# An encoder layer with 16 experts: where the prompt's matmuls stand between the sample's

## The reference, cut to what matters

```python
SEQ, DEC_SEQ, D_MODEL = 256, 1024, 1024          # prompt tokens, sample tokens
N_EXPERTS, CAPACITY_FACTOR, EXPERT_FF = 16, 2, 2048

def _expert_choice_ffn(h, w_router, w_e_gate, w_e_up, w_e_down):
    B, S, D = h.shape
    T = B * S
    cap = CAPACITY_FACTOR * T // N_EXPERTS       # 32 prompt rows, 128 sample rows per expert
    ht = h.reshape(T, D)
    aff = jax.nn.softmax((ht @ w_router).astype(jnp.float32), axis=-1)
    gate_vals, idx = lax.top_k(aff.T, cap)
    xe = ht[idx]
    hid = jax.nn.silu(jnp.einsum('ecd,edf->ecf', xe, w_e_gate)) * jnp.einsum('ecd,edf->ecf', xe, w_e_up)
    ye = jnp.einsum('ecf,efd->ecd', hid, w_e_down) * gate_vals[..., None].astype(h.dtype)
    out = jnp.zeros((T, D), ye.dtype).at[idx.reshape(-1)].add(ye.reshape(-1, D))
    return out.reshape(B, S, D).astype(h.dtype)

def _layer(x, ...):
    h = _rmsnorm(x, norm_mix)
    proj = h @ w_in
    ...
    o_a = _gla_branch(...)                       # gated linear attention, both directions
    o_b = _gqa_branch(...)                       # grouped-query attention
    merged = jax.nn.sigmoid(z_a) * (o_a @ w_o_gla) + jax.nn.sigmoid(z_b) * (o_b @ w_o_att)
    x = x + merged @ w_out
    x = x + _expert_choice_ffn(_rmsnorm(x, norm_ffn), w_router, w_e_gate, w_e_up, w_e_down)
    return x
```

## Time and profile before

| | us |
|---|---|
| median of 3 runs | 3241.99 |
| lowest and highest | 3238.33, 3242.4 |
| the profiled execution: its own time | 3243.4 |
| its span, first to last instruction | 3241.8 |
| TensorE busy in the span | 3032.2 (94%) |
| VectorE, ScalarE busy | 1706.0 (53%), 1518.9 (47%) |
| SP's loads and stores, share of the 16 DMA engines' span | 43.9% |
| sample matmuls, high weights times rows | 578.2, 395 ns each |
| prompt matmuls on the rows | 236.1, 383 ns each |

### The profile page before, as it was taken

One profiled execution on the slowest core, in us unless ns is written; L12 is line 12 of the kernel. 1 busy time (PEld: TensorE's weight loads), 2 busy tenths in 40 slices (PEclk: granted clock), 3 DMA queues, 4 the chain that ended last, 5 costly groups with the idle time before them and its releaser, 6 DMA issues. The chain is left out here.

```text
span 3241.8 us, 51622 instructions
## 1 busy us (share of the span) xinstructions
PE 3032.2 (94%) x19370; PEld 2396.0 (74%) x19370; DVE 1706.0 (53%) x1733; ACT 1518.9 (47%) x1647; POOL 564.5 (17%) x732
## 2 busy tenths in 40 slices
PE   7999998899987799988885999999999999999998
PEld 5888886777776689967773777777777777777776
DVE  3101000544443299942337666666766766666665
ACT  4211111455543166631443565656656655566554
POOL 0038883012210000000101000111110001111100
PEclk9999998999998899999996999999999999999999
DMA  4324322232325300034436778888877787888874
GB/s 147 131 97 142 117 89 95 92 108 86 95 73 194 110 14 20 13 120 173 143 122 226 273 278 304 282 286 297 293 272 279 281 304 277 289 299 286 277 278 151
DMA packets 196508, 600.83 MB, mean 185 GB/s; under 512 B 15360, under 2 KB 45712, under 8 KB 196432
## 3 DMA queue, kind: packets, MB, share of 16 engines
q1 hardware_dynamic: 165952, 507.51, 43.9%
q0 software_dynamic: 21760, 74.99, 7.8%
q10 hardware_dynamic: 8720, 17.30, 1.5%
HBM read 522.33 MB, written 77.33 MB: 185 GB/s over the span
## 5 line engine op out<-in xcount | busy, mean ns | idle before, releaser
L1932 DVE TENSOR_TENSOR ex_w_lo<-ex_w_raw,ex_w_hi 128x2048 fp32r<-128x2048 f32 x384 | 879.7, 2291 | 451.5 <-ACT ex_w_hi L1887 451.5
L1887 ACT ACTIVATE ex_w_hi<-ex_w_raw 128x2048 fp32r<-128x2048 f32 x381 | 730.0, 1916 | 469.5 <-PE ex_ps_s L2019 469.3
L2019 PE MATMUL ex_ps_s<-ex_w_hi,ex_xS 128*128 128x512 f32 x2048 | 578.2, 395 | 0.0
L2019 PEld LDWEIGHTS ex_ps_s<-ex_w_hi,ex_xS 128*128 128x128 f32 x2048 | 375.9, 188 | 99.4 <-issue 26.3
L2019 PE MATMUL ex_ps_s<-ex_w_lo,ex_xS 128*128 128x512 f32 x1024 | 316.4, 390 | 0.0
L2019 PE MATMUL ex_ps_s<-ex_w_hi,ex_hidS 128*128 128x512 f32 x1024 | 307.9, 403 | 0.0
L1873 POOL DMA_INDIRECT y<-ex_ye_s,ex_rows_y x16 | 43.5, 2718 | 1147.4 <-DVE ex_ye_s L1975 1147.4
L2030 PE MATMUL ex_ps_p<-ex_w_raw,ex_xP 128*32 128x256 f32 x4096 | 236.1, 383 | 0.0
L109 PE MATMUL pj_ps_tok<-pj_w_hi,act_hl 128*128 128x512 f32 x560 | 219.5, 392 | 8.9 <-DVE pj_w_lo L406 8.9
L2019 PEld LDWEIGHTS ex_ps_s<-ex_w_lo,ex_xS 128*128 128x128 f32 x1024 | 192.2, 188 | 41.4
L111 PE MATMUL pj_ps_tok<-pj_w_hi,act_hl 128*128 128x512 f32 x560 | 218.6, 390 | 0.0
(11 more groups left out here) (293 smaller groups left out, 5117.7 us busy)
## 6 DMA issues: line engine op xcount, KB each, us to landing
ex_w_raw<-w_e_gate SPq DMA_DIRECT2D x128, 1024.0 KB, 11.3
ex_w_raw<-w_e_up SPq DMA_DIRECT2D x128, 1024.0 KB, 12.1
ex_w_raw<-w_e_down SPq DMA_DIRECT2D x128, 1024.0 KB, 8.7
proj_t<-pj_stage SPq DMA_DIRECT2D x60, 256.0 KB, 2.0
pj_w_raw<-w_cols ACTq DMA_DIRECT2D x7, 2048.0 KB, 9.2
z_w_raw<-w_z SPq DMA_DIRECT2D x16, 512.0 KB, 3.8
gate_logits<-gl_z_stage SPq DMA_DIRECT2D x32, 256.0 KB, 2.1
pj_w_raw<-x SPq DMA_DIRECT2D x10, 512.0 KB, 4.0
```

Of the source, the lines that this page charges most:

```text
L1887: act.activation(whl[0][:, j % NHL], raw[:, j % NRAW], ACT.Copy).then_inc(w_hi, 1)
L1932: dve.tensor_tensor(whl[1][:, j % NHL], raw[:, j % NRAW], whl[0][:, j % NHL].bitcast(F32), ALU.subtract).then_inc(w_lo, 1)
L2019: mm = pe.matmul(ps_s[:, s, c:c + 512], x(part, k), whl[w][:, j % NHL, kk, c:c + 512], start=k == 0 and part + w == 0, stop=k == 2 * PU - ...
```

## The change

TensorE's prompt batch of phases 1, 3 and 5 moves from the start of its phase to its end, behind the fourth sample unit, where the batch of the next even phase (phase 0 of the next expert after phase 5) comes next. On VectorE the product or sum of that batch moves behind that of the sample. No instruction is added or removed, and the code of SP, GpSimd and ScalarE stays as it is, with the same values to wait for.

```diff
--- before.py
+++ after.py
@@ -1956,15 +1956,6 @@
                             if j == 22 + r and not last:
                                 turn_low(h + 4 + r + 1, xS[:, 1, 4 * r:4 * r + 4], (7 + r) % 2, xS[:, 0, 4 * r:4 * r + 4])
                         f = j // PU
-                        if f % 2 == 1 and j % PU == 0:
-                            dve.wait_ge(p_full, CR + PHASES * e + f + 1)
-                            dve.wait_ge(act_p, CR + 3 * e + f // 2 + 1)
-                            if f < 4:
-                                dve.wait_ge(turned, CR + q + f // 2)
-                                dve.tensor_tensor(hP[:], sgP[:], ps_p[:, 1, 0:QW], ALU.mult).then_inc(dve_p, 1)
-                            else:
-                                dve.scalar_tensor_tensor(out=yP[:], in0=ps_p[:, 1, 0:QW], scalar=gate[1][:], in1=yP[:],
-                                                         op0=ALU.mult, op1=ALU.add).then_inc(dve_p, 1)
                         if f % 2 == 1 and j % PU == PU - 1:
                             dve.wait_ge(u_done, CR + UNITS * e + j + 1)
                             dve.wait_ge(act_s, CR + 3 * e + f // 2 + 1)
@@ -1974,6 +1965,14 @@
                             else:
                                 dve.scalar_tensor_tensor(out=yS[:], in0=ps_s[:, 1], scalar=gate[0][:], in1=yS[:],
                                                          op0=ALU.mult, op1=ALU.add).then_inc(dve_s, 1)
+                            dve.wait_ge(p_full, CR + PHASES * e + f + 1)
+                            dve.wait_ge(act_p, CR + 3 * e + f // 2 + 1)
+                            if f < 4:
+                                dve.wait_ge(turned, CR + q + f // 2)
+                                dve.tensor_tensor(hP[:], sgP[:], ps_p[:, 1, 0:QW], ALU.mult).then_inc(dve_p, 1)
+                            else:
+                                dve.scalar_tensor_tensor(out=yP[:], in0=ps_p[:, 1, 0:QW], scalar=gate[1][:], in1=yP[:],
+                                                         op0=ALU.mult, op1=ALU.add).then_inc(dve_p, 1)
 
                 dve.wait_ge(turned, CR + 1)
                 dve.tensor_copy(xP[:].rearrange("p k t -> p (k t)"), ps_t[:, 0, 0:KC * CP]).then_inc(turn_out, 1)
@@ -2033,17 +2032,22 @@
 
                 def body(e, last):
                     q = XT + TURNS * e
+
+                    def prompt_phase(f):
+                        pe.wait_ge((act_p, dve_p)[f % 2], CR + 3 * e + f // 2)
+                        if f == 0:
+                            pe.wait_ge(turn_out, CR + q - 2)
+                        if f >= 4:
+                            pe.wait_ge(turn_out, CR + q + 3 * (f - 4) + 1)
+                            prompt(e, f, lambda k, c: hidP[:, f - 4, k % 2, CP * (k // 2):CP * (k // 2) + CP])
+                        else:
+                            prompt(e, f, lambda k, c: xP[:, k])
+
                     for j in range(UNITS):
                         f, i = j // PU, j % PU
                         if i == 0:
-                            pe.wait_ge((act_p, dve_p)[f % 2], CR + 3 * e + f // 2)
-                            if f == 0:
-                                pe.wait_ge(turn_out, CR + q - 2)
-                            if f >= 4:
-                                pe.wait_ge(turn_out, CR + q + 3 * (f - 4) + 1)
-                                prompt(e, f, lambda k, c: hidP[:, f - 4, k % 2, CP * (k // 2):CP * (k // 2) + CP])
-                            else:
-                                prompt(e, f, lambda k, c: xP[:, k])
+                            if f % 2 == 0:
+                                prompt_phase(f)
                             pe.wait_ge((act_s, dve_s)[f % 2], CR + 3 * e + f // 2)
                             if f == 0:
                                 pe.wait_ge(turn_out, CR + q)
@@ -2070,6 +2074,8 @@
                             if r:
                                 pe.wait_ge(turn_out, CR + q + 6 + r - 1)
                             turn_x(r)
+                        if f % 2 == 1 and i == PU - 1:
+                            prompt_phase(f)
 
                 for j in range(2):
                     pe.wait_ge(x_in[j], 16)
```

## The result

| | before | after |
|---|---|---|
| median of the runs, us | 3240.36 (4 runs) | 3289.45 (4 runs) |
| ratio, 95% interval | | 1.0145 [1.0129, 1.0161] |
| span of the profiled execution, us | 3241.8 | 3288.8 |
| mean granted clock of TensorE | 0.972 | 0.967 |

The change makes the kernel 49 us slower, 47.0 us in the profiled executions. No change was forecast (3243, range 3228 to 3257), so the forecast is wrong: the time lies 32 us above its range, and the rise is seven times the 6.5 us that it would have called no change.

The account below looks back on a forecast made before the run. TensorE's own instruction stream was taken to bound the experts. Expert 0 at -0.7, 14 borders together +2.8, the last border -0.55 and the end -0.8 gave +0.75 us on 3243.4; median forecast 3243, range 3228 to 3257.

Parts of the forecast that it names:

- A switch: On TensorE, going from sample to prompt matmuls and back: 0.35 us each, 47 of them saved, 16.5 us.
- a seam: On TensorE, the join between two prompt batches now back to back: taken as 0 us, bounds 0 to 0.35.
- The 0.8 at the end: At the kernel's end, 0.48 us of VectorE work after the last matmul rather than 1.28: -0.8 us.
- The rival in which a seam costs as much as a switch: Joins of prompt batches on TensorE save nothing: total +7 us, 3249; chance 4%.
- What the change gives on TensorE: Prediction's step on TensorE's gain: 96 prompt sections become 49, 16.5 us go; VectorE's displaced work is hidden; end -0.8 us.
- a sign that something is wrong: TensorE's granted clock falling after a stand, listed among observations that would prove the forecast wrong; no size given.
- s, the stand per border: TensorE's wait for late loads at each expert border: 1.25 us taken, total -16.75 + 14 s.
- the chain by units 6 and 7: At a border, third load through ScalarE and VectorE conversions makes TensorE's unit late: 0.5 us (0.2 to 0.8).
- The stand at the prompt batch: After a border, TensorE waits for the eighth load before the last quarter of phase 2's prompt batch: 1.05 us.
- the scatter's 3.8: At a border, the scatter of the old expert's rows beside four loads delays their landing by 3.8 us.
- the gather's 3.3: At a border, the gather of new rows delays the landing of the next four loads by 3.3 us.
- the faster rival: Border loads come in time, wait up to 0.5 us per border: total -10 to -17, 3225 to 3232; chance 27%.

Follow-up runs that it names:

- hidden_first: Changed kernel, with ScalarE and VectorE taking out the last transposed hidden quarter ahead of unit 19's weight conversion: 3235.75 us, ratio 0.9973 to the kernel before.
- move_1_3: Kernel before with only the prompt batches of phases 1 and 3 moved, phase 5's left at its phase's start: 3233.14 us, ratio 0.9964.
- move_5: Kernel before with only the prompt batch of phase 5 moved: 3301.17 us in one run, 56 more than before on that chip.
- filler: Changed kernel with nine unread matmuls added before TensorE's wait for hidden rows in phase 5: 3273.58 us, ratio 1.0083 to the kernel before.
- no_scatter: Changed kernel with the hidden quarter taken out first and without the scatters of the experts' outputs: 3222.77 us in one run.
- old_order_both: Kernel before, no batch moved, with the hidden quarter taken out first and weight buffers freed one by one: 3244.0 us, ratio 0.9995.

## Why the prediction was wrong

**What bounds the kernel, and the gain.** Right. A switch costs 0.36 us (30.61 - 30.25), where 0.35 was taken, and a seam nothing: 47 x 0.36 + 0.8 = 17.7 us. The 0.8 at the end shows as well: from TensorE's last matmul to the end of the span it is 14.24 us, before it was 15.07. The rival in which a seam costs as much as a switch is refuted by the 3.48 us from batch to batch, also across the loop's branch. That agrees with the rule on a change of tiling mode in the Trainium skill, "TensorEngine Tiling (Array Packing)", section Key Properties. It doesn't prove it: sample and prompt matmuls also differ in data type (a rounded form of float32, and float32 itself), and no run changes one without the other.

**The step that failed.** In "What the change gives on TensorE" I asked what hides the operations that the move puts elsewhere, the low half behind VectorE's wait for instance. I didn't ask what the moved batch itself had been hiding. Of the three batches one, phase 5's, stood between the last transpose of hidden rows and the first unit that reads them. Moved away, it leaves 2.3 us of wait in each of 16 experts; TensorE's conditions at that place are in the code (`turn_out` for f of 4 or more), and the ready time 2012.13 against 2010.29 in the trace of before. The prediction said that at pairs away from a border TensorE waits for nothing, and its sum has no term for it; the wait stands in phase 5, ahead of the border pair. Phases 1 and 3 have no such cover to lose: phase 3 reads rows that were long ready, and nothing is transposed in them. hidden_first, move_1_3 and move_5 show it from three sides.

**The clock.** Listed only as a sign that something is wrong, without a price. It was 1.6 us in 13 of 16 experts, about 20 us of the 47. filler shows that it comes with the idle time: with matmuls in the gap it stays away. It isn't the loads, as the sixteenth expert has none beside it.

**The loads at a border.** Late loads do make TensorE stand there, but of the two stands only the smaller came. s, the stand per border, was taken as 1.25 us; the runs show 0.3 to 0.9, 0.54 in the mean (29.57 against 29.03), nearly all of it the chain by units 6 and 7 that was sized at 0.5. The stand at the prompt batch, sized at 1.05, did not occur: at the border shown TensorE came 0.6 later and the eighth load 0.5 us earlier than forecast, and on average that load took 30.7 us and not 32.2. Of the terms of that sum the scatter's 3.8 holds (30.7 against 26.9 in no_scatter); the gather's 3.3 was too large (30.7 against 29.2 at the border without one, 1.5). The estimate by "DMA: Bandwidth & Descriptors" in the Trainium skill, section Anatomy of one DMA, 24 us for the eight loads and the row transfers, was further off than that sum.

**The sum.** Without the wait it comes out: hidden_first at 0.9973 is 8.8 us under its before (its interval leaves 5 to 12). The formula of the forecast, -16.75 + 14 s, gives -9.2 with s = 0.54, where the forecast had +0.75. So the forecast's sum was short of one term, 16 x 2.3 + 13 x 1.6 = some 58 us (56 by the two ratios, 1.0145 and 0.9973). Without that wait the time would have come out at the faster rival (3225 to 3232, given 27%): 0.9973 of 3240.4 is 3231.6. That is still in the range, but it isn't the middle, 3243.

## What to carry to other kernels

A block of work that is moved takes with it what it covered. For each place it leaves, list what the next instruction there waits for, and compare when that was ready with when the block before the gap ended: such a wait is in no list while it is covered. And where a late operand stands behind a long conversion on two in-order queues, moving the short operation ahead cost nothing here (old_order_both) and was worth more than the move itself.

## What the runs showed of the hardware

An idle time of TensorE of 2.0 us (1.8 in the sixteenth expert), in a stretch otherwise busy from end to end, was followed by matmuls at 1.2 GHz in 13 of 16 experts with all batches moved, and in 4 of 16 with only phase 5's moved, after an equal wait. What decides between them stays open. It is not the load on the DMA engines: the stretches in which it fell have a DMA share of 1.02 or, in the sixteenth expert, 0.01, and one in which it stayed up has 1.03. With nine spare matmuls in the gap it never fell, and 2.2 us of useless work made an expert 1.5 us shorter.
